# Padding the rows of the matmul operands and the slots of the weight ring in a three-layer block on one core

## The reference, cut to what matters

```python
def swiglu(x, w_in, w_out):                       # w_in 1024 x 5632, w_out 2816 x 1024
    gate, up = jnp.split(x @ w_in, 2, axis=-1)
    return (jax.nn.silu(gate) * up) @ w_out

x = x + 0.5 * rms_norm(swiglu(rms_norm(x, g), w_in, w_out), post_g)     # first model, twice
x = x + rms_norm(concat([attention(q, k, v), ssm(u)]) @ w_mix_out, g)   # its mixer
x = layer_norm(ALPHA * x + 0.5 * swiglu_2(x, gate, up, down), g, b)     # second model, twice a layer
x = layer_norm(ALPHA * x + concat([pool(u), hgrn(q, f, v, g)]) @ w_out) # its mixer
```

## Time and profile before

| | |
|---|---|
| median of 3 runs | 3057.91 us |
| the profiled execution | 3054.1 us |
| its span, first to last instruction | 3052.3 us |
| mean granted TensorE clock | 0.973 of full speed |
| TensorE matmul busy | 2965.3 us (97%) |
| weight loads busy | 2429.0 us (80%) |
| VectorE, ScalarE, GpSimd busy | 44%, 33%, 13% |
| mean DMA | 85 GB/s |

### The profile page before, as it was taken

One profiled execution on the slowest core, in us unless ns is written; L12 is line 12 of the kernel. 1 busy time (PEld: TensorE's weight loads), 2 busy tenths in 40 slices (PEclk: granted clock), 3 DMA queues, 4 the chain that ended last, 5 costly groups with the idle time before them and its releaser, 6 DMA issues.

```text
span 3052.3 us, 32618 instructions
## 1 busy us (share of the span) xinstructions
PE 2965.3 (97%) x13432; PEld 2429.0 (80%) x13432; DVE 1330.1 (44%) x1783; ACT 1009.4 (33%) x1345; POOL 395.0 (13%) x427
## 2 busy tenths in 40 slices
PE   8999989899999999999999999999999999899998
PEld 6888876578888788887887888778887788788886
DVE  5553267654342433334655333343333455543333
ACT  4232234453232332323333332233332333343222
POOL 3110056311110000011231000100001113100010
PEclk9999989899999999999998999999999999899998
DMA  4222211122222233222211322223222221122321
GB/s 148 97 97 97 96 51 63 22 76 90 97 98 96 76 104 97 97 91 74 77 56 56 104 97 97 85 75 106 97 98 86 69 85 54 63 96 91 104 83 69
DMA packets 76019, 260.41 MB, mean 85 GB/s; under 512 B 11728, under 2 KB 11856, under 8 KB 75856
## 3 DMA queue, kind: packets, MB, share of 16 engines
q1 hardware_dynamic: 75872, 258.34, 25.7%
HBM read 255.03 MB, written 2.10 MB: 84 GB/s over the span
## 4 chain that ended last, share of the span: by engine, by line
PE 90%; DVE 6%; issue 2%; ACT 1%; POOL 1%; DMA 0%; SPq 0%; DVEq 0%; ACTq 0%; POOLq 0%
PE bank L324 24%; PE bank L326 24%; PE bank L325 24%; PE bank L338 2%; PE bank L339 2%; PE bank L344 2%; PE bank L682 2%; PE bank L435 2%; PE bank L445 1%; DVE Hl L1292 1%; PE bank L373 1%; PE bank L374 1%; PE bank L377 1%; PE bank L607 1%; DVE wlo L1284 1%
## 5 line engine op out<-in xcount | busy, mean ns | idle before, releaser
L1284 DVE TENSOR_TENSOR wlo<-wraw,whi 128x1024 fp32r<-128x1024 f32 x474 | 592.6, 1258 | 1078.8 <-ACT whi L793 1078.5
L324 PE MATMUL bank<-Hh,whi 128*128 128x512 f32 x2320 | 910.9, 393 | 11.2 <-DVE wlo L1284 9.3
L325 PE MATMUL bank<-Hh,wlo 128*128 128x512 f32 x2320 | 906.3, 391 | 0.0
L326 PE MATMUL bank<-Hl,whi 128*128 128x512 f32 x2320 | 906.0, 391 | 0.0
L793 ACT ACTIVATE whi<-wraw 128x1024 fp32r<-128x1024 f32 x479 | 502.4, 1057 | 1212.6 <-PE bank L326 1160.5
L324 PEld LDWEIGHTS bank<-Hh,whi 128*128 128x128 f32 x2320 | 437.6, 189 | 104.7 <-issue 11.3
L326 PEld LDWEIGHTS bank<-Hl,whi 128*128 128x128 f32 x2320 | 437.1, 188 | 91.0
L325 PEld LDWEIGHTS bank<-Hh,wlo 128*128 128x128 f32 x2320 | 437.4, 189 | 89.7
L324 PE MATMUL bank<-Ah,whi 128*128 128x512 f32 x1056 | 417.9, 396 | 0.0
L325 PE MATMUL bank<-Ah,wlo 128*128 128x512 f32 x1056 | 417.0, 395 | 0.0
L326 PE MATMUL bank<-Al,whi 128*128 128x512 f32 x1056 | 417.0, 395 | 0.0
(11 more groups left out here) (258 smaller groups left out, 2472.4 us busy)
## 6 DMA issues: line engine op xcount, KB each, us to landing
wraw<-weights SPq DMA_DIRECT2D x479, 512.0 KB, 3.5
X<-x_t SPq DMA_DIRECT2D x8, 256.0 KB, 7.2
y_t<-X SPq DMA_DIRECT2D x8, 256.0 KB, 2.0
Y<-masks SPq DMA_DIRECT2D x1, 512.0 KB, 8.9
MUb<-ssm SPq DMA_DIRECT2D x1, 256.0 KB, 8.1
tmp<-ssm SPq DMA_DIRECT2D x1, 256.0 KB, 3.8
zsum<-attention SPq DMA_DIRECT2D x1, 256.0 KB, 4.9
MUb<-attention SPq DMA_DIRECT2D x1, 256.0 KB, 6.2
```

The costliest lines, as they stand in the source:

```text
L324: pe.matmul(b, sh, mh, start=start, stop=False)
L325: pe.matmul(b, sl, mh, start=False, stop=False)
L326: signal(pe.matmul(b, sh, ml, start=False, stop=stop), keys)
L1284: dve.tensor_tensor(wlo[:, u % NH, :], wraw[:, u % NR, :], f32(whi[:, u % NH, :]), SUB).then_inc(*S.done("weights_lo", ("lo", u)))
```

## The change

Rows and slots get unused bytes behind them, so that the next one starts at another distance from a multiple of 512:

- Hh and Hl: 8 values (32 bytes) behind each of their 8 rows; a row starts 2080 bytes after the one before.
- whi and wlo: 20 values (80 bytes) behind each of their 3 slots; a slot starts 4176 bytes after the one before. The 8 tiles within a slot stay 512 bytes apart.
- Ah and Al: 4 values (16 bytes) behind each of their 22 rows; a row starts 2064 bytes after the one before.
- X, wraw, Y and the mixers' own tensors keep their rows.

The views that the rest of the kernel uses have the same shapes as before, and no instruction is added, taken away or moved. The small tensors behind wlo lie 1024 bytes further on. To keep the start of the arena where it is, `sp5` (16 rows of 16 values for the set-up of the state-space mixer) leaves the fixed part and lies over row 4 of Y. The new starts are 17536 (Hh), 34176 (Hl), 63104 (whi), 75648 (wlo), 120640 (Ah) and 166048 (Al).

```diff
-    Hh = at("Hh", [P, KD, T], F32R)
-    Hl = at("Hl", [P, KD, T], F32R)
+    Hh = at("Hh", [P, KD, T + 8], F32R)[:, :, 0:T]
+    Hl = at("Hl", [P, KD, T + 8], F32R)[:, :, 0:T]
     wraw = at("wraw", [P, NR, 1024], F32)
-    whi = at("whi", [P, NH, 1024], F32R)
-    wlo = at("wlo", [P, NH, 1024], F32R)
+    whi = at("whi", [P, NH, 1024 + 20], F32R)[:, :, 0:1024]
+    wlo = at("wlo", [P, NH, 1024 + 20], F32R)[:, :, 0:1024]
...
-    sp5 = at("sp5", [P, 16, 16], F32)
...
-    Ah, _ = ar("Ah", [P, NF, T], F32R)
-    Al, _ = ar("Al", [P, NF, T], F32R)
-    Y, _ = ar("Y", [P, KD, T], F32)
+    Ah, _ = ar("Ah", [P, NF, T + 4], F32R)
+    Al, _ = ar("Al", [P, NF, T + 4], F32R)
+    Ah, Al = Ah[:, :, 0:T], Al[:, :, 0:T]
+    Y, o_y = ar("Y", [P, KD, T], F32)
+    sp5, _ = ar("sp5", [P, 16, 16], F32, o_y + 4 * T * 4)
```

## The result

The changed kernel takes 3085.82 us (median of 4 runs, 3084.49 to 3091.49) where the kernel before takes 3055.85 us (4 runs). The ratio is 1.0101, with a 95% interval of 1.0088 to 1.0113: 30 us slower. The forecast was 22 us slower.

What follows compares the result with a forecast made beforehand. Bound by the number of matmuls times each one's time in an unbroken TensorE stream. H +29 us and A -7 us on 3054.1 give 3076; the runs' median lies 3.8 us higher, so 3080 us, range 2993 to 3125.

Steps and rivals of the forecast that it cites:

- addresses alone make the matmuls slower: Whole kernel: changed addresses act only through the time per 512-column matmul, +22 us in all; slower had chance 0.54.
- the writing engines, DMA and sp5: ScalarE and VectorE writes to shifted rows, untouched transfers and sp5 over row 4 of Y: all costed at nothing.
- 226.5 ns was a good state and not a middling one: Matmuls on Hh and Hl: a long series at one distance settles at 226.5 ns; unsettled ones take 233 ns.
- Rival A: Matmul streams: the average distance is a good one, so the kernel gets faster, -50 us, 3008 us; chance 0.33.
- H: The 8256 matmuls on Hh, Hl or with a weight slot moving: 226.5 to 230 ns each, +29 us.
- settled for perhaps half of them: Matmuls on Hh and Hl: distances hold for 12 matmuls, about half settled, hence 230 ns, between 226.5 and 233.
- A: The 3216 matmuls on Ah, Al, yh and yl: 233.3 to 231 ns each, -7 us.
- The inference under it: All matmuls: weight load and moving stream hinder each other at full clock, by their addresses; 176 us of 3054 lost.
- third of that effect: Rival A's smaller version: 222 ns for A, 225.5 for H, -44 us, against -97 us for half way down to 213.
- Rival B: Moving rows starting off a 64-byte boundary take 33 pieces, not 32: +44 us beyond the forecast, 3124 us; chance 0.12.
- Rival C: Nothing changes: the 6.8 ns belong to the part of memory, or the mean falls near 228.4; 3058 us, chance 0.13.
- the unsettled stretches of the old trace: Matmuls right behind others: 6 steps at 233 ns before 9 at 227, taken as showing that mixed distances cost more.

## Why the prediction was right

**That addresses alone make the matmuls slower: right.** The chain, the counts and the idle times left nothing else, and the writing engines, DMA and sp5 cost nothing, as worked out. The windows have 778 matmuls where 783 were forecast, and 433 where 433 were; the steps differ from row to row, and rows at one distance are alike.

**That 226.5 ns was a good state and not a middling one: right, and this gave the sign.** The argument came from the earlier trace rows, where the same matmul takes 233 and 236 ns. No distance in the changed kernel and no place in any other brought a 512-column matmul below 226.6 ns. Rival A needed an average under 228.4; it is 232.1.

**The size.** H was taken at 230 ns and came to 232.1, so 8256 x 3.5 = 29 us should have been about 40. The step that failed is "settled for perhaps half of them". Most distances never settle at 226.7: the stream repeats a pattern at 232 to 234 ns from the first matmul to the last, as slots 1 and 2 of the kernel with padded slots show. A was taken at 231 ns and came to 231.7, -5 us for -7. And 4.4 us came back in all other matmuls and the waits behind them, which the sum had not counted; TensorE's idle time fell by 5.4 us, from 3052.3 - 2965.3 = 87.0 to 3083.0 - 3001.4 = 81.6. The misses partly cancel, which leaves 30 us for 22; that it came so near owes something to luck.

**The inference under it: wrong.** I read the loss as the weight load and the stream getting into each other's way. Cutting the load to 2 columns does not remove the loss but raises it. What the runs show is that every 512-column matmul of these products loses 13.3 ns or more at full clock, and that the distance, the place modulo 32 bytes and what ran before shift that loss. What makes it stays open.

**Rival A** was priced higher than its words: its "third of that effect" is -44 of -97 us, nearer a half. **Rival B** is refuted as it stands: rows 32 bytes off a multiple of 64 cost nothing at distance 0. It was right that some boundary counts; rows 16 bytes off cost 3.3 to 6.6 ns there. **Rival C's** part of the memory is refuted by the moved arena. The Trainium skill, in "SBUF — State Buffer", section "Specifications (TRN2)", gives lines of 16 bytes; the rows at 16 bytes past a multiple of 32 start on such a line and are dearer all the same, 230.0 to 233.3 for 226.7 ns. And the 216 ns that the Trainium skill gives for 512 columns in "TensorE: Matmul & The Clock Gate", section "Back-to-back issue gap", as the gap of a single matmul without the share of its weight load, is reached by none of the float32r matmuls here; the best is 10 ns above it.

**Left open:** what makes the 13 to 20 ns, whether the load instruction or the output has a part in them, why they are least at distance 0 on multiples of 32 bytes, and what chooses between the three rhythms of one layout. The runs give it per matmul and by address, not by mechanism. The kernels with the common shifts, the 4-byte steps and the changed loads ran once each, though with thousands of matmuls in each run.

## What to carry to other kernels

When a kernel is bound by a stream of matmuls, compare the time from start to start between groups of the same shape: two tensors that differ by 3% with nothing else different are a difference in address, and moving the one to the residue of the better one is free (here 20 us, 0.6%). Spreading rows over many alignments averages over good and bad; find the good one and put everything there. And before a change replaces one state by a mixture, ask whether the present state is better or worse than the mixture: here the unsettled stretches of the old trace gave the sign, though not the mechanism.

## What the runs showed of the hardware

- A float32r matmul of 512 columns with its own weight load takes 226.7 ns in a stream at 2.4 GHz at best, 13.3 more than its columns; one of 384 columns takes 173.3, also 13.3 more. At 1.2 GHz it takes 425 ns, with no such loss.
- The time depends on the distance between moving row and stationary tile, which was read modulo 256 bytes (a wlo slot 256 bytes further on, modulo 512, than its whi slot still settles near 227): 226.7 at 0, 229 to 230 at 64, 232 to 234 at most multiples of 32, up to 236.8 at distances that are no multiple of 16.
- At distance 0, a common place 16 bytes past a multiple of 32 costs 3.3, 4.4 or 6.6 ns more, one of the three for a whole stage in one and the same kernel, and 32 bytes past a multiple of 64 costs nothing.
- Such times are patterns that repeat, and they depend on what went before: after a change of slot, distance 0 needs 46 ns in all to fall back to 226.7.
- A weight load of 2 columns beside the stream gives 231.1 ns wherever it starts, more than one of 128 columns at distance 0.
- Times of VectorE and ScalarE do not depend on these alignments: 1258 and 1057 ns with slots at 0, 80 and 160 bytes.
